# Where a small stage runs: compressing the prompt's keys and values inside a projection

## The reference

```python
def compress_rows(x, pe, w1, w2):          # x [N, Tk, KH=4, Dh=64]; blocks of 32 rows, one every 16
    n_cmp = (Tk - CMP_LEN) // CMP_STRIDE + 1                   # 31 for the prompt
    chunks = x[:, :n_chunk * CMP_STRIDE].reshape(N, n_chunk, CMP_STRIDE, KV_HEADS_B, HEAD_DIM)
    w1r = w1.reshape(CMP_RATIO, CMP_STRIDE, HEAD_DIM, CMP_HIDDEN)
    proj = jnp.einsum('ncjkd,rjde->rncke', chunks, w1r)
    hid = jnp.einsum('jd,jde->e', pe, w1)                      # the same for every block
    for r in range(CMP_RATIO):
        hid = hid + proj[r, :, r:r + n_cmp]
    return jnp.einsum('ncke,ed->nckd', jax.nn.silu(hid), w2)

# layer b of the prompt
q_c, q_r, rows, wrows, gates, z = project_b(rms_norm(x, norm_g), w_in, ...)
k_cmp = rms_norm(compress_rows(rows[:, :, 0], pe[0], w1[0], w2[0]), k_gain)
v_cmp = compress_rows(rows[:, :, 1], pe[1], w1[1], w2[1])
```

## Time and profile before

| | |
|---|---|
| median of 3 runs | 1239.73 us |
| time of the profiled execution | 1240.55 us |
| its span, first to last instruction | 1238.5 us |
| PE busy | 1177.7 us (95%), 7934 instructions |
| DVE, ACT, POOL busy | 460.7, 395.3, 301.6 us |
| mean granted TensorE clock | 0.991 |

### The profile page before, as it was taken

One profiled execution on the slowest core, in us unless ns is written; L12 is line 12 of the kernel. 1 busy time (PEld: TensorE's weight loads), 2 busy tenths in 40 slices (PEclk: granted clock), 3 DMA queues, 4 the chain that ended last, 5 costly groups with the idle time before them and its releaser, 6 DMA issues. The chain is left out here.

```text
span 1238.5 us, 20994 instructions
## 1 busy us (share of the span) xinstructions
PE 1177.7 (95%) x7934; PEld 763.7 (62%) x7934; DVE 460.7 (37%) x1205; ACT 395.3 (32%) x924; POOL 301.6 (24%) x418
## 2 busy tenths in 40 slices
PE   7999999999899999799999997999998999999998
PEld 4676676577587773345445565555566868686543
DVE  2333333000255641343222202766663353536410
ACT  4111111111366520232112312766663343424200
POOL 0666665000000000068434000545450000000000
PEclk9999999999999999999999997999999999999999
DMA  7333334485120798215678970502007846554901
GB/s 268 136 136 135 146 147 161 175 311 175 60 94 2 275 389 321 89 67 209 219 254 318 372 142 34 166 2 69 2 1 175 234 129 215 162 178 124 218 22 51
DMA packets 89021, 197.61 MB, mean 160 GB/s; under 512 B 9898, under 2 KB 41562, under 8 KB 87770
## 3 DMA queue, kind: packets, MB, share of 16 engines
q1 hardware_dynamic: 88922, 196.27, 47.9%
HBM read 185.56 MB, written 73.28 MB: 209 GB/s over the span
## 5 line engine op out<-in xcount | busy, mean ns | idle before, releaser
L464 PE MATMUL bank<-region,la_hT 128*128 128x512 f32 x640 | 284.1, 600 | 0.0
L464 PEld LDWEIGHTS bank<-region,la_hT 128*128 128x128 f32 x640 | 173.2, 275 | 93.9 <-issue 44.4
L1351 PE MATMUL bank<-region,lb_oT 128*128 128x512 f32 (+1 forms) x448 | 185.2, 569 | 0.4 <-DVE lb_oT L268 0.4
L1351 PEld LDWEIGHTS bank<-region,lb_oT 128*128 128x128 f32 x448 | 83.5, 190 | 88.4 <-issue 83.9
L1624 PE MATMUL bank<-cs_chunks_turned,region 128*128 128x252 f32 x512 | 121.7, 383 | 3.2 <-DVE cs_chunks_turned L1689 2.4
L1624 PEld LDWEIGHTS bank<-cs_chunks_turned,region 128*128 128x128 f32 x512 | 93.7, 192 | 17.3 <-DVE cs_chunks_turned L1689 4.5
L1689 DVE COPY cs_chunks_turned<-bank 64x512 f32<-64x512 f32 x64 | 43.7, 683 | 68.9 <-PE bank L1608 68.7
L1691 ACT ACTIVATE cs_chunks_turned<-bank 64x512 f32<-64x512 f32 x64 | 37.9, 593 | 94.8 <-PE bank L1608 94.7
L540 POOL TENSOR_TENSOR pa_swapped<-pa_normed,pa_tables 128x256 f32<-128x256 f32 (+1 forms) x60 | 50.2, 855 | 69.1 <-DVE pa_normed L555 69.1
L2031 POOL TENSOR_SCALAR ab_probs<-ab_probs,ab_rec,lb_gates 128x128 f32<-128x128 f32 (+3 forms) x96 | 58.1, 619 | 33.9 <-DVE ab_rec L2077 33.7
L495 ACT ACTIVATE pa_squares<-bank 128x512 f32<-128x512 f32 (+1 forms) x30 | 16.0, 533 | 155.9 <-PE bank L464 148.3
(11 more groups left out here) (341 smaller groups left out, 1789.5 us busy)
## 6 DMA issues: line engine op xcount, KB each, us to landing
region<-in_a_w_in SPq DMA_DIRECT2D x9, 2048.0 KB, 8.0
out_new_dil_s<-in_cache_dil SPq DMA_DIRECT2D x8, 2032.0 KB, 13.4
region<-in_b_w_in SPq DMA_DIRECT2D x6, 2048.0 KB, 7.9
region<-in_cache_dil SPq DMA_DIRECT2D x11, 1024.0 KB, 14.1
sa_cache<-in_cache_dil SPq DMA_DIRECT2D x9, 1024.0 KB, 11.6
lb_qp<-in_cache_nsa_paged SPq DMA_DIRECT2D x32, 256.0 KB, 4.4
region<-in_cache_nsa_paged SPq DMA_DIRECT2D x32, 256.0 KB, 4.2
sb_sel_keys<-in_cache_nsa_paged SPq DMA_DIRECT2D x64, 128.0 KB, 3.4
```

Source lines behind the costliest of these rows:

```text
L464: ins = nc.tensor.matmul(U[u.v % 3][:, :], permuted(hT[:, k, :], u.g, u.t), W[:, u.c % 2, k, :], start=(k == 0), stop=(k == KC - 1))
L1351: ins = nc.tensor.matmul(U[u.v % 3][:, 0:n], hT[:, k, u.t * P:(u.t + 1) * P], weight_rows(u, k), start=(k == 0), stop=(k == KC - 1))
```

## The change

The compression loses its stage. Its PE instructions stand between and behind the last units of the projection, those of ACT beside the takings-out of the same units, those of DVE and POOL behind their work for the projection. In full:

- From unit 31 on (`START` is unit 30, the first of chunk 6) a function `compress(i)` follows each unit: one turn of the pages behind each of units 31 to 36; behind unit 36 also the turns of z, position rows and gains; behind unit 37 a turn, the 32 matmuls of the position rows, the last turn and the keys' `hidden`; behind unit 38 the values' `hidden` and the keys' `tokens`; behind unit 39 the values' `tokens` and `turn_keys`.
- The order of chunk 7 is the sample rows first, then the four tiles.
- SP: the pages come in two DMAs over 128 partitions and go ahead of the cache copies of step 5; w2, the position rows and the gains follow these copies and have a semaphore of their own (`cmp_small`); w1 comes, still after chunk 6, in two DMAs over 128 partitions in place of four over 64.
- Banks: pages are turned in bank 3, `hidden` uses 4, `tokens` 5, the position rows' products and z 6, small turns 7. The projection's tables and work buffers become one tensor `work`, and the compression's buffers are laid over it (`later`).

```diff
-        for t in range(TILES + 1):
+        for t in range(TILES + 1) if c < NC - 1 else (TILES, *range(TILES)):
...
+        C = Compress(S, "cp_", [2], weights, [pages], [S.lasting_sem("cp_pages0")], landed, KC_P, VC_P,
+                     (S.banks[3], S.banks[4], S.banks[5]), ctx, make=later)
+        START = len(units) - 10
...
-                        copy_kept(S, sp, 3, [c])
-                        copy_kept(S, sp, 2, [c])
+                        if c < NC - 3:
+                            copy_kept(S, sp, 3, [c])
+                            copy_kept(S, sp, 2, [c])
...
                 sp.wait_ge(s_u, 5 * (NC - 2))
                 sp.wait_ge(S.s_rows_out, 16 * TILES)
-                for b in range(SEQ // PAGE):
-                    lo = 64 * (b % 2)
-                    sp.dma_start(pages0[lo:lo + 64, b // 2, :, :], back[b, :, :, 0:512]).then_inc(S.lasting_sem("cp_pages0"), 16)
+                for b in range(2):
+                    sp.dma_start(pages[b][:, :, :], back[b, :, :, 0:512]).then_inc(S.lasting_sem("cp_pages0"), 16)
+                for which in (3, 2):
+                    copy_kept(S, sp, which, [NC - 3])
+                load_small_weights(S, sp, weights)
                 sp.wait_ge(s_lin, 5)
                 sp.dma_start(A["scratch_gates"], GATES[0:NS, TILES, :]).then_inc(s_gs, 16)
                 sp.wait_ge(s_u, 5 * (NC - 1))
-                load_compress_weights(S, sp, weights)
+                load_hidden_weights(S, sp, weights)
...
+                def compress(i):
+                    if 1 <= i < 8:
+                        C.turn(pe, i - 1)
+                    if i == 6:
...
+                        pe.wait_ge(S.lasting_sem("cmp_small"), 64)
...
+                    if i == 7:
+                        pe.wait_ge(s_petc, 2)
+                        pe.wait_ge(s_zc, 1)
+                        pe.wait_ge(S.lasting_sem("cmp_w"), 32)
+                        for rm in range(16):
+                            for kv in range(2):
...
+                        C.turn(pe, 7)
+                        for quarter in range(4):
+                            C.hidden(pe, 0, quarter)
...
+                    if i == 8:
+                        for quarter in range(4):
+                            C.hidden(pe, 1, quarter)
+                        C.tokens(pe, 0)
...
+                    if u.v >= START:
+                        compress(u.v - START)
+                for i in range(2):
+                    ending(i)
...
+                    i = u.v - START
+                    if 1 <= i < 8:
+                        C.copy_out(act, i - 1, 1)
...
+def load_hidden_weights(S, sp, weights):
+    A, s_w, w1 = S.dram, S.lasting_sem("cmp_w"), weights[0]
+    for kv in range(2):
+        src = A["b_cmp_w1"][0, kv].rearrange("(m a) d e -> (a d) m e", a=2)
+        sp.dma_start(w1[:, kv, :, :, :].rearrange("p r m e -> p (r m) e"), src).then_inc(s_w, 16)
...
-            compress_prompt_stage(S, KC_P, VC_P, weights, pages[1], T_z, T)
```

More of the change, by code:

```diff
@@ L1179, in layer_a, with project_b_stage @@
         sample_a_stage(S, T, oT, W_out, ring, W)
-def project_b_stage(S, hT, W, QP, KT, ROWS, WINR, Z, GATES, T_rows, T_z, T, weights, pages0):
+def project_b_stage(S, hT, W, QP, KT, ROWS, WINR, Z, GATES, T_rows, T_z, T, weights, pages, KC_P, VC_P):
     nc, A = S.nc, S.dram
@@ L1232, in project_b_stage, with landed @@
         TP, TR = S.banks[3:5], S.banks[5:7]
+        w1, _, pe_rows, peT, pe_hid, k_gains, k_gain = weights
+        s_zt, s_zc, s_pet, s_petc, s_ph, s_phc, s_pht, s_pre = (
+            S.sem("pp_" + n) for n in ("z_turned", "z_copied", "turned", "copied", "hidden", "hidden_copied", "hidden_turned", "hidden_done"))
+        HB_, SIDE = S.banks[6:8]
+        def landed(pe, it, s_pg):
+            pe.wait_ge(s_pg[0], 32)
+        C = Compress(S, "cp_", [2], weights, [pages], [S.lasting_sem("cp_pages0")], landed, KC_P, VC_P,
+                     (S.banks[3], S.banks[4], S.banks[5]), ctx, make=later)
+        hid_rows = later([2 * NS, HID])
+        START = len(units) - 10
         with S.block() as block:
@@ L1334, in _ @@
                         rows.ready(pe, u.t)
-                    if u.t == 0 and u.c == NC - 1:
+                    if u.first and u.c == NC - 1:
                         pe.wait_ge(s_w_last, 16)
-                    elif u.t == 0:
+                    elif u.first:
                         pe.wait_ge(s_w[u.c % 2], 16 * (u.c // 2 + 1))
@@ L1545, in _, with __init__ @@
                 dve.wait_ge(s_q, 8 * NB)
+                for x in range(6):
+                    C.copy_out(dve, x, 0)
+                dve.wait_ge(s_pet, 1)
+                nc.vector.tensor_copy(peT[:, :], SIDE[:, 256:288]).then_inc(s_petc, 1)
+                nc.vector.tensor_copy(k_gain[:, :], SIDE[:, 384:385]).then_inc(s_petc, 1)
+                C.copy_out(dve, 6, 0)
+                dve.wait_ge(s_ph, 1)
+                nc.vector.tensor_copy(hid_rows[:, :], HB_[0:2 * NS, 0:HID]).then_inc(s_phc, 1)
+                C.copy_out(dve, 7, 0)
+                dve.wait_ge(s_pht, 1)
+                nc.vector.tensor_copy(pe_hid[:, :], SIDE[:, 288:288 + 2 * NS:NS]).then_inc(s_pre, 1)
+                C.key_squares(dve, 0)
+                C.key_scale(dve, 0)
+                C.keep(dve, 0)
 class Compress:
-    def __init__(self, S, pfx, items, weights, pages, s_pg, landed, KC_T, VC, banks, ctx, head=0, extra=(None, None)):
+    def __init__(self, S, pfx, items, weights, pages, s_pg, landed, KC_T, VC, banks, ctx, head=0, extra=(None, None), make=None):
         def sb(name, shape):
+            if make:
+                return make(shape)
             return ctx.enter_context(S.nc.sbuf_tensor(pfx + name, shape, F32))
@@ L1769, in dve_step, with load_small_weights @@
             self.key_scale(dve, y // 2 - 1)
[L1772 to L1779, removed]
+def load_small_weights(S, sp, weights):
+    A, s_w = S.dram, S.lasting_sem("cmp_small")
+    _, w2, pe_rows, _, _, gains, _ = weights
     sp.dma_start(w2[:, :, :], A["b_cmp_w2"][0].rearrange("v e d -> e v d")).then_inc(s_w, 16)
@@ L2683, in layer_b @@
             QP = [early, sb("qp1", [P, 2, 4, TOK], inner)]
[L2685 removed]
             KC_P = sb("kc_p", [P, 1, 2, 64], inner)
             VC_P = sb("vc_p", [64, 1, 256], inner)
[L2688 removed]
+            project_b_stage(S, oT, W_in, QP, KT, ROWS, WINR, Z, GATES, T_rows, T_z, T, weights, pages[1], KC_P, VC_P)
             attend_b_stage(S, QP, KT, ROWS, WINR, KC_P, VC_P, GATES, Z, oT, pT, pages[0])
```

115 lines of the change are left out of this document (46 added, 69 removed).

## The result

The changed kernel takes 1230.36 us (median of 6 runs, 1227.82 to 1231.72) where the kernel before takes 1239.62 us (6 runs): ratio 0.991, 95% interval 0.9891 to 0.9928, so it is faster by 8.9 to 13.5 us. The ratio makes it 11.2 us, the two medians alone 9.3. In a second comparison, with the last of the experiments, it is 1229.8 us against 1242.31 us, ratio 0.9907, interval 0.9886 to 0.9928. The forecast was 1227.3 us, in a range of 1224.5 to 1233 us.

A forecast was written before the change was run, and what follows sets the result against it. PE's waits and lowered clock in the compression bound the kernel: 14.3 + 1.0 + 2.6 = 17.9 us replace 29.8, with 0.5 of clock 12.4 us off 1239.73, giving 1227.3 us; range 1224.5 to 1233 us.

The forecast's parts named there:

- The sum as a whole: Projection's last matmul to attention's first: 14.3 + 1.0 + 2.6 = 17.9 us replace 29.8, with the clock 12.4 us less.
- PE's own work, 14.3 us: Compression's turns, position rows' product, `hidden` and keys' `tokens`, moved among projection units at full clock: 14.3 us, between 13.8 and 15.3.
- The wait before the fifth turn, 1.0 us: PE waits before the fifth turn of pages for ACT's copy, delayed by sample copies: about 1.0 us, bounds 0 and 1.5.
- w1, no wait: Before the position rows' product: w1 over 128 partitions lands in time, wait 0, bounds 0 and 2.3 us.
- T: End of chunk 6's last unit, when w1 is issued; 725.36 us in the trace before, w1 needed about T + 10.9.
- The pages, at 704 us at the latest: Pages, issued about 695.9 us ahead of step 5's copies, land by 704 us; needed at 709.6, 5 us to spare.
- rival C: Pages held up by following cache copies until 721.5 us; PE stands 11.9 us in chunk 6; 3.4 us slower; chance 0.05.
- The first barrier without an heir: Barrier at the compression's start: its 3.4 us standstill vanishes, as SP's gates, issued right behind w1, land early.
- The tail, 2.6 us: Behind the last tile: values' `tokens`, their copy, the keys' turn, `keep` and the barrier before the attention, 2.6 us as before.
- The attention's start, 0.5 us: Attention's first 3 us, before at clock 0.50, partly regain speed if the clock stays up: 0.5 us, between 0 and 1.5.
- B: w1 over 128 partitions no faster; PE waits 2.3 us, clock may fall; 2.3 to 6.2 us given back; chance 0.18.
- D: Some 15 hand-overs to ACT and DVE each cost PE 0.5 us; 7.5 us given back, 1234.8 us; chance 0.07.

The follow-up runs named there:

- the run with the later copies: Changed kernel with ACT's copies of the samples' keys and values three units later; 1232.54 us, ratio 0.9929 to the kernel before.
- The run with the copies first: Changed kernel with the two cache copies of step 5 issued ahead of the pages again; 1244.56 us, ratio 1.0025 to the kernel before.
- the kernel with the broken tiles: Changed kernel with later sample copies, w1's products inside chunk 7's third tile, values' `tokens` and `turn_keys` inside the last; 1226.9 us, ratio 0.988.

## Why the prediction was right, point by point

- *The sum as a whole.* It had 17.9 us in place of the 29.8 us of the gap, 11.9 us less, and 0.5 us of clock. By the stretch it is 10.8 us. The mechanism is the one of the text: each experiment with a part undone changes the wait that the text names for it, though not always by the size that it gives. The new order of chunk 7 was not undone by itself. The upper end of the forecast's own range is wrong by its own terms: 1.0 more work, 0.5 more wait and no clock make 1229.3 us, not 1229.5.
- *PE's own work, 14.3 us.* The stretch is 63.65 us; less the 44.66 us of chunks 6 and 7 (740.40 - 695.74), the two waits and the tail, 14.6 us are left, inside 13.8 to 15.3. The product took 3.69 us, not 3.2: the 50 ns a record came from its last 1.3 us alone.
- *The wait before the fifth turn, 1.0 us.* 1.05 us. But the text priced it as a loss that could be had back; by the run with the later copies it isn't, since PE then stands 1.1 us longer for w1. Two waits in a row on one path have one price.
- *w1, no wait.* This term was mis-sized, within its bounds of 0 and 2.3 us. The load was put at T + 7.8 us by the load of chunk weights of the same size and partitions; the row of the landing after, and the rate from 730 to 737 us (last column GB/s):

```profile
DMA to landing us min/median/max: 6.4/8.1/9.8
```

```profile
730.00:737.00 7.00, 6.92 (x35) 6.02 (x36) 1.09 (x4) 1.90 (x5) 0.00 (x0) 1.00 1.01 280
```

  The second transfer was issued at about 729.0 and landed at 738.8 us, T + 11.2 with T = 727.6 us, at some 290 GB/s and not at 385. Of the 3.4 us between T + 7.8 and T + 11.2, 1.3 are the later issue of the second transfer and 2.1 its longer landing, 9.8 us where the chunk weights took 7.7. The 3 us of slack in the sum were not there; PE waited 0.47 us. What holds the rate at 290 GB/s to 128 partitions, the 512-byte runs or something else, no run shows. The Trainium skill's rule ("SBUF — State Buffer", section "Door 1: The DMA port swizzle") stood closer with 196 and 328 GB/s for 1 MiB to 64 and 128 partitions; the runs here have 188 and 290.
- *The pages, at 704 us at the latest.* They were issued at 697.5 and 698.2 us and landed 8.1 us later (median), at about 706 us, and PE came at 711.2 us; chunk 6 starts 1.6 us later here than in the trace that the 704 us came from, so the 5 us to spare are right. The run with the copies first made rival C the case: its 11.9 us of wait are 11.88 there. That its loss of 3.4 us is a measured 3.1 is luck in part. C set 15.8 us of wait and clock against a gain of 12.4 us; the stretch of that run, 77.76 us, is 14.1 us longer than the changed kernel's and 3.3 longer than before's, so the clock cost some 2.2 us and not 3.9, and the gain lost was 10.8.
- *The first barrier without an heir.* Right: only the barrier before the attention is left, with 1.39 us of idle time where it had 1.20, and nothing stands for the first one's 3.4 us. That this part could be had without the move (3.6 us, with the clock's share) the text didn't say.
- *The tail, 2.6 us.* It is 2.85 us; of the difference 0.2 are the longer idle time at the barrier, 1.39 for 1.20.
- *The attention's start, 0.5 us.* It gave 0. The granted clock still fell, as the busy times of the changed kernel show:

```profile
761.00:762.00 1.00, 0.99 (x4) 0.64 (x6) 0.98 (x4) 1.00 (x1) 1.00 (x2) 0.68 0.00 0
762.00:763.00 1.00, 1.00 (x4) 0.47 (x3) 0.24 (x1) 0.25 (x1) 0.24 (x1) 0.50 2.74 975
```

  The 2.1 us from PE's stop to the fall, read from one standstill, are no measure for others: in the run with four transfers over 64 partitions PE stood for 3.70 us and the clock stayed at 1.00.
- *The rivals.* B was not the case, and where it was made the case its sum was short: 2.3 to 6.2 us given back were forecast, some 7 us were measured with four transfers over 64 partitions, behind a wait of 3.70 us and not 2.3. D was not: no wait for a copy but the one named and the 0.55 us in the tail, which was there before.
- *The rest.* The median of 1230.36 us is 3.1 us above the forecast: 1.6 us are the terms above (10.8 for 12.4), 1.5 us lie outside the stretch, where the clock's falls at other borders differ from run to run. That they are chance was not shown by itself; by the ratio of the same runs the gain is 11.2 us, and in the second comparison 11.6, and then nothing is missing.

## What to carry to other kernels

A short stage of many hand-overs gains inside its neighbour's long stream: the chains of copies and norms cost nothing where a tile of PE's work lies over them. What more polish in place would have brought no run shows; better loads alone brought 3.6 us of the 10.8. Inside the stream what decides is when the loads count as landed, so the order of DMA issues and the partitions that they reach have to be settled together with the order of the matmuls; here the move with the copies first gained nothing. And of two waits in a row on the same path, price the pair, not each.

## What the runs showed of the hardware

- Loads with the same 512-byte runs moved 188 to 193 GB/s to 64 partitions (193 in the kernel before) and 289 GB/s to 128; packets of 2 KB (the two transfers over 128) made no difference to the latter, 291 GB/s.
- Two loads of 512 KB issued right behind two cache copies landed after 22.9 us, issued ahead of them after 8.1 us; the 512 packets that are by number and size those of the loads moved, behind the copies, only from 715 us on, some 17 us after the issue.
- A wait of PE of 3.70 us left the clock at its upper level in one execution, one of 4.34 us did not in another; ahead of the attention 2.2 us with 0.28 us of work were followed by a fall, 1.57 us of standstill in the kernel with the broken tiles were not.
